# First queries of the attention computed inside the last z tile, and the decays of the second and third quarter two score pairs later

## The reference

```python
def odd_mixer(h_ctx, h_lat, w_in, w_out, conv_w, conv_b, wq, wk, wv, w_if, b_if, norm_g, skip):
    xm, zg = jnp.split(h @ w_in, [ML_WIDTH], axis=-1)          # 2048 + 2048 columns
    xcv = jax.nn.silu(centred_dwconv(xm, conv_w, conv_b))
    q, k, v = headwise(xcv, wq), headwise(xcv, wk), headwise(xm, wv)   # 4x4 blocks
    hm = prefix_bidir(mlstm_scan, (q, k, v), forward, backward)
    return ((head_norm(hm, norm_g) + skip * xcv) * jax.nn.silu(zg)) @ w_out

# one chunk of mlstm_scan; b is the running sum of log f
dmat = where(mask, b[t] - b[s] + log_i[s], -inf)
s    = (q @ k.T) * exp(dmat - m_t)
num  = s @ v + (carried state);  den = sum(s) + (carried state)
h    = num / max(|den|, exp(-m_t))
```

## Time and profile before

| | |
|---|---|
| time, three runs | 2762.35, 2759.66, 2761.38 us; median 2761.38 |
| the profiled execution's own time | 2756.0 us |
| its span | 2754.4 us |
| TensorE busy | 2570.5 us (93% of the span) |
| VectorE, ScalarE, GpSimd busy | 1534.2 (56%), 829.9 (30%), 982.6 (36%) us |
| chain that ended last | TensorE 70%, VectorE 8%, ScalarE 4%, issue 2%, DMA 2%, GpSimd 1% |
| mean granted TensorE clock | 0.974 |
| attention (1905 to 2500 us) | TensorE busy 568.90 of 595.00 us |

### The profile page before, as it was taken

The page is one execution under the profiler, slowest core; times in us unless marked ns, Lnnn a source line. Parts: engine busy times, 40 slices in busy tenths (PEclk is TensorE's granted clock), DMA queues, the critical chain, the costliest instruction groups (busy, mean ns, idle before and its releaser), DMA issues.

```text
span 2754.4 us, 37624 instructions
## 1 busy us (share of the span) xinstructions
PE 2570.5 (93%) x13319; PEld 1990.4 (72%) x13319; DVE 1534.2 (56%) x2362; ACT 829.9 (30%) x997; POOL 982.6 (36%) x1163
## 2 busy tenths in 40 slices
PE   7897789999989998989999999999999989999998
PEld 3777754445445667878877877778888889887787
DVE  4677755887875224433237655866455554646510
ACT  2425634362552113222122111213233242322210
POOL 0139967887800000011233333444334433331000
PEclk9999999999999999999999999999999999999999
DMA  8312220101105776351132333474121220315421
GB/s 298 109 65 99 98 74 24 58 23 50 50 28 191 250 223 215 82 193 35 43 84 83 124 126 116 167 248 146 43 104 62 104 81 31 125 42 168 131 92 46
DMA packets 257472, 298.09 MB, mean 108 GB/s; under 512 B 34960, under 2 KB 217528, under 8 KB 256960
## 3 DMA queue, kind: packets, MB, share of 16 engines
q1 hardware_dynamic: 201568, 206.60, 23.6%
q10 hardware_dynamic: 51168, 73.04, 7.4%
q0 software_dynamic: 4608, 16.78, 1.8%
HBM read 203.09 MB, written 93.29 MB: 108 GB/s over the span
## 4 chain that ended last, share of the span: by engine, by line
PE 70%; DVE 8%; ACT 4%; issue 2%; DMA 2%; POOL 1%; ACTq 0%; DVEq 0%; SPq 0%; POOLq 0%
PE ps L135 61%; PE ps L1315 6%; DVE xc_part L2440 1%; PE ps L973 1%; ACT arena L1510 0%; ACT L1510 0%; PE ps L1320 0%; DVE arena L520 0%; PE ps L1268 0%; POOL decays L2839 0%; PE ps L1146 0%; DVE arena L2204 0%; DMA y_chunks<-arena 0%; DVE s_scan_tmp L2152 0%; DVE arena L2154 0%
## 5 line engine op out<-in xcount | busy, mean ns | idle before, releaser
L135 PE MATMUL ps<-h_full,weights 128*128 128x512 f32 (+1 forms) x1152 | 424.1, 529 | 21.0 <-DMA weights<-in_e_w_in 8.1
L135 PE MATMUL ps<-h_part,in_weight_parts 128*128 128x512 f32 (+1 forms) x1920 | 413.8, 376 | 14.2 <-DVE arena L2357 6.7
L135 PEld LDWEIGHTS ps<-h_part,in_weight_parts 128*128 128x128 f32 x1920 | 337.8, 190 | 85.7 <-issue 13.6
L135 PEld LDWEIGHTS ps<-h_full,weights 128*128 128x128 f32 x1152 | 220.8, 193 | 217.4 <-issue 204.5
L135 PE MATMUL ps<-v_part,p_part 128*128 128x512 f32 x1248 | 296.7, 397 | 0.1
L135 PEld LDWEIGHTS ps<-v_part,p_part 128*128 128x128 f32 x1248 | 235.4, 191 | 49.8 <-issue 0.9
L135 PE MATMUL ps<-q_part,xc_part 128*128 128x256 f32 x1920 | 246.9, 287 | 14.7 <-DVE v_part L2440 10.8
L135 PEld LDWEIGHTS ps<-q_part,xc_part 128*128 128x128 f32 x1920 | 236.5, 194 | 16.4 <-DVE v_part L2440 11.5
L135 PE MATMUL ps<-arena,weights 64*16 64x128 f32 (+2 forms) x896 | 180.7, 395 | 16.5 <-ACT arena L1510 14.4
L1315 PE MATMUL ps<-wo_part,mx_part 128*128 128x512 f32 x768 | 183.8, 400 | 6.9 <-DVE mx_part L2440 6.3
L1315 PEld LDWEIGHTS ps<-wo_part,mx_part 128*128 128x128 f32 x768 | 145.6, 191 | 41.3 <-issue 6.5
(11 more groups left out here) (398 smaller groups left out, 4198.0 us busy)
## 6 DMA issues: line engine op xcount, KB each, us to landing
weights<-in_e_w_in SPq DMA_DIRECT2D x32, 512.0 KB, 4.2
weights<-in_o_w_in SPq DMA_DIRECT2D x32, 512.0 KB, 4.5
s_out_maps<-arena ACTq DMA_DIRECT2D x16, 640.0 KB, 2.9
arena<-s_out_maps SPq DMA_DIRECT2D x16, 640.0 KB, 4.9
ml_xcv<-arena ACTq DMA_DIRECT2D x16, 640.0 KB, 3.0
xc_full<-ml_xcv SPq DMA_DIRECT2D x4, 2560.0 KB, 9.2
xm_tiles<-ml_xm SPq DMA_DIRECT2D x16, 640.0 KB, 3.9
weights<-in_mod_w POOLq DMA_DIRECT2D x17, 512.0 KB, 5.3
```

What stands on the lines that cost most here:

```text
L135: return nc.tensor.matmul(o, lhsT, rhs, start=(k == 0), stop=(k == n - 1))
```

## The change

Three things are moved; no arithmetic is added or taken away.

1. TensorE computes `queries(0, 0)`, 12 matmuls of 256 columns, inside `output_gate(15)`, ahead of its last two blocks k = 6 and 7 (12 matmuls of 512 columns). Before, they followed the tile. ScalarE and VectorE evict these two query halves ahead of their work on tile 15, where before they did it behind that tile's stores. `queries(0, 1)` still follows the tile. To allow it the helper functions are defined ahead of the loops, and the wait for the last z tile's eviction moves to the first `value_sums`.
2. In every head `decays(i, 1)` moves from `first_queries` to behind the third pair of quarter 0.
3. In every head `decays(i, 2)` moves from behind the fifth pair of quarter 0 to behind the third pair of quarter 1.

```diff
--- before.py
+++ after.py
@@ TensorE, output_gate(m)
                 for k in range(DT):
+                    if m == MT - 1 and k == 6:
+                        pe.wait_ge(*past("z_ev", 14))
+                        queries(0, 0)
@@ TensorE, value_sums
+                if u0 and j == 0:
+                    pe.wait_ge(*past("z_ev", MT))
@@ TensorE, behind the z tiles
-            pe.wait_ge(*past("z_ev", 14))
-            queries(0, 0)
             queries(0, 1)
-            pe.wait_ge(*past("z_ev", MT))
             head(0, False)
@@ ScalarE
             for m in range(MT):
+                if m == MT - 1:
+                    queries_high(0, 0)
                 output_gate(m)
...
             def first_queries(i):
-                queries_high(i, 0)
+                if not (isinstance(i, int) and i == 0):
+                    queries_high(i, 0)
                 queries_high(i, 1)
                 act.wait_ge(*past("ce_ready", i + 1))
                 nc.scalar.activation(cE, cE, ACT.Exp).then_inc(sem("cx_ready"), 1)
                 decays(i, 0)
-                decays(i, 1)
...
                 for p in range(NPR - 1):
                     value_high(i, p + 2)
                     weights_high(i, 0, p)
+                    if p == 2:
+                        decays(i, 1)
                 queries_high(i, 2)
                 weights_high(i, 0, NPR - 1)
-                decays(i, 2)
                 value_high(i, 6)
                 for p in range(NPR):
                     value_high(i, p + 7)
                     weights_high(i, 1, p)
+                    if p == 2:
+                        decays(i, 2)
@@ VectorE
             for m in range(10, MT):
+                if m == MT - 1:
+                    for h in range(2):
+                        query_low(0, 0, h)
                 gate_tile(m)
...
                 for q in range(2):
                     for h in range(2):
-                        query_low(i, q, h)
+                        if q or not (isinstance(i, int) and i == 0):
+                            query_low(i, q, h)
```

More of the change, by code:

```diff
@@ L1164, in gate_rows_spread @@
                 last.then_inc(sem("gates_spread"), 1)
[L1166 to L1187, removed]
             def slot(i, *x):
@@ L1300, in head @@
                 weight_sums(i, 3, 1)
-            pe.wait_ge(*past("z_ev", 14))
-            queries(0, 0)
+            mixer_input(1, 0)
+            gate_sums(0, 0)
+            with pe.Fori(1, MT // 2 - 1) as i:
+                mixer_input(i, 1)
+                gate_sums(i - 1, 1)
+                mixer_input(i + 1, 0)
+                gate_sums(i, 0)
+            mixer_input(MT // 2 - 1, 1)
+            gate_sums(MT // 2 - 2, 1)
+            for m in range(MT):
+                output_gate(m)
+                if m == 9:
+                    pe.wait_ge(*past("z_ev", 9))
+                    pe.wait_ge(*past("rows_ready", 2))
+                    pe.wait_ge(*past("em_ready", 1))
+                    for j in range(LBLK):
+                        nc.tensor.transpose(ps[:, 5, 64 * j:64 * j + 64], rA[0:64, P * j:P * j + P], ident[0:64, 0:64])
+                    pe.wait_ge(*past("yr_ready", 1))
+                    for b in range(NBLK):
+                        nc.tensor.transpose(psf[:, 6 * BANK + 64 * b:6 * BANK + 64 * b + 64], rB[0:64, P * b:P * b + P], ident[0:64, 0:64])
+                    pe.wait_ge(*past("tr_ready", 1))
+                    mm(ps[:, 2, 0:40], ones[0:64, :], TR.rearrange("p d h j -> p (d h j)"), 0, 1).then_inc(sem("rows_t"), 1)
             queries(0, 1)
-            pe.wait_ge(*past("z_ev", MT))
             head(0, False)
@@ L1727, in maps_high, with queries_high @@
                 high(CH, CR, "c_high")
+            def queries_high(i, q):
+                for h in range(2):
+                    act.wait_ge(*past("lo_mm", slot_done(i, "q", q, h)))
+                    high(Qs[0][:, q % 2, 2 * h:2 * h + 2].rearrange("p k t -> p (k t)"), slot_bank("q", q, h), "vq_high", MD ** -0.5)
             for m in range(MT):
+                if m == MT - 1:
+                    queries_high(0, 0)
                 output_gate(m)
@@ L1767, in value_high @@
                 high(Vs_[0][:, bs, P * k:P * k + P], slot_bank("v", n)[:, 0:w].rearrange("p (b c) -> p b c", c=P), "vq_high")
[L1769 to L1772, removed]
             def decays(i, q):
@@ L2468, in out_weights_split, with query_low @@
                     out_weights_low(k)
+            def query_low(i, q, h):
+                dve.wait_ge(*past("vq_high", 20 * i + EVICTED["q", q, h]))
+                o, hi = (Qs[x][:, q % 2, 2 * h:2 * h + 2].rearrange("p k t -> p (k t)") for x in (1, 0))
+                V.scalar_tensor_tensor(out=o, in0=slot_bank("q", q, h), scalar=MD ** -0.5, in1=hi.bitcast(F32), op0=ALU.mult, op1=ALU.subtract).then_inc(sem("vq_ev"), 1)
             for m in range(10, MT):
+                if m == MT - 1:
+                    for h in range(2):
+                        query_low(0, 0, h)
                 gate_tile(m)
@@ L2475, in _ @@
                     maps_low(0)
[L2477 to L2480, removed]
             def first_queries(i, then=()):
```

## The result

The changed kernel takes 2737.95 us (median of 4 runs, 2736.18 to 2742.87), beside 2760.52 for the kernel before on the same chip (4 runs, 2758.59 to 2762.35). The ratio is 0.9922, 95% interval 0.9907 to 0.9938: 21.5 us won (17 to 26). The forecast was 16.2 us won and 2745.2, range 2742 to 2752. The profiled execution of after took 2739.68 us. One later run of the kernel before, 4288.94 us at a mean granted clock of 0.556, is a run in a slow state and is left out of every comparison; all others were fast.

What follows compares the result with a forecast made beforehand. TensorE, busy 93% of the span, was taken as the bound, so only its waits and low clock could be won. 2.6 + 10.75 + 0 + 2.83 = 16.2 us off 2761.4 gave 2745.2, range 2742 to 2752.

Steps and rivals of the forecast that it cites:

- The start: Start of head 0: value slot 2 starts 2.6 us earlier, despite a new 4.0 us wait for value rows.
- Rival 1: The start of head 0 gives nothing, TensorE's wait only turning to value rows: 13.6 us won, 2747.8; chance 0.12.
- (b) waits: TensorE's waits for value slot 6 before quarter 1's second score pair, every head; all four go, 10.75 us.
- Rival 4: The (b) waits stay, slot 6 waiting for something the decays hid; only the start is won, 2758.8; chance 0.06.
- Decays of quarter 1: Moved ahead of value slot 5, with a table load in heads 1 to 3: cost 0, 0.76 us left.
- Rivals 3 and 5: Table switch in heads 1 to 3 costs more, 14.6 us won, chance 0.05; moved decays stand bare, +15 us, 0.04.
- (c) waits: TensorE's 1.28 us before quarter 1's first pair, heads 1 to 3, until a query half is evicted; forecast to stay.
- The clock: Two slow score pairs behind (b) waits return to 3.14 us: 2.83 us won, bounds 2.83 and -4.2.
- rival 2: The clock isn't won back, or drops elsewhere: 13.4 or 9.2 us won, 2748.0 to 2752.2; chance 0.13.

Runs made afterwards that it cites:

- start_d1: The kernel before with parts 1 and 2 of the change together, decays of quarter 2 left as before: 2756.03 us, ratio 0.9989.
- p_d2: The kernel before with only part 3 of the change, decays of quarter 2 moved in every head: 2742.40 us, ratio 0.9941.
- fill_b: The kernel before with 16 unread matmuls of 256 columns into an unused bank in each (b) wait: 2752.97 us, ratio 0.9980.
- p_null: The kernel before, unchanged, timed against itself and profiled a second time: 2758.68 us, ratio 1.0000.
- p_again: The changed kernel, unchanged, timed once more beside the kernel before: 2741.12 us, ratio 0.9929.
- p_again2: The changed kernel, unchanged, timed yet again beside the kernel before: 2736.91 us, ratio 0.9924.
- c_only: The kernel before with VectorE evicting both query halves of quarter 2 ahead of the second mixing product, heads 1 to 3: 2761.64 us, ratio 1.0014.
- x2: The changed kernel with c_only's edit, plus half of each head's last value sums ahead of the waiting weight sums: 2730.49 us, 0.9895 to the kernel before.
- p_d1: The kernel before with only part 2 of the change, decays of quarter 1 moved: 2757.64 us, ratio 0.9994.

## Why the prediction was wrong in size and right in kind

1. *The start, 2.6 us.* Right, step by step: a new wait of 3.86 us (4.0 forecast) for value rows that land after 5.1 us (5.3), value slot 2 earlier by 2.8 in the profile, 3.0 by start_d1. Rival 1 (nothing) would have given start_d1 a ratio of 1.0000, just outside its interval; the traces refute it more clearly, by 2.8 to 2.9 us in every execution with parts 1 and 2.
2. *The (b) waits, 10.75 us.* Right that all four go, in after and in p_d2, but worth 11.7: I added up the idle times, and each wait also cost the 0.25 us by which the next group would have started ahead of the end of the one before. Rival 4 is refuted.
3. *Decays of quarter 1, cost 0.* Right, with 0.75 us left where 0.76 was forecast, and no loss behind the table load. Rivals 3 and 5 are refuted: no wait ahead of slots 5 or 10, (c) waits still 1.28.
4. *The clock, 2.83 us with 2.83 as its upper bound.* This step failed: "With the (b) waits gone I take the two slow pairs back to 3.14: 1.49 + 1.34". The (b) waits cost 5.5 us of clock (3.0 to 8.0, fill_b). The single execution that I read had a low clock behind two waits of four, and p_null, the same code, had it behind three, at up to 2.35 us a time. I had even noted that equal waits met the clock differently, and used that only as a reason for a smaller gain: rival 2 lowers the term, and nothing raises it. The price could have been bounded from above by the rows at hand: four waits each followed by a slow pair at 1.34 to 1.49 us, twice 2.83 or 5.7. What is shown is that 2.83 was too small to be a bound; how much too small is open between the profiles' mean of 3.65 and 8.0.
5. *The base.* The forecast of 2745.2 stood on a median of three runs, 2761.4; 62 later runs of the same kernel gave medians of 2758.3 to 2758.6. That is 2.9 us of the 7.25 by which the forecast was off. The other 4.4 lie in the gain, 20.7 against 16.2: 2.7 in the clock (by fill_b; 0.8 by the profiles' mean), 1.0 in the tails of the (b) waits, 0.4 in the start, and 0.4 left over. That is inside the intervals (p_d2 and start_d1 add up to 19.3, each give or take 3 to 4), so whether the parts help one another stays open.

The extra 3.2 us that the profile of after showed in the value sums is no part of this: the profiles of p_again and p_again2 have them slow in heads 0 to 2, at ratios of 0.9929 and 0.9924.

## What to carry to other kernels

A wait on TensorE costs its length, here 0.25 us more than its idle time shows, and, in some executions, the low clock behind it. Price it from the start of one group to the start of the next. For the clock, take that price from several executions or from an experiment that fills the wait, and let the range reach up to every such wait paying in full. Before removing a wait, ask what sets its end and that of the next one: c_only took 3.9 us out in front of waits whose ends were fixed, and lost 3.9; x2 won nothing in head 3, where another engine's chain ended the next wait. A forecast of an absolute time needs more than three runs of the kernel before.

## What the runs showed of the hardware

- Work that nobody reads made the kernel 5.5 us faster (fill_b), by holding the granted clock up across four waits of 2.5 to 3.3 us; 0.55 to 1.36 us of idle time in each did no harm.
- A wait of 1.57 us was followed by the low clock more often than not. In after, the last value sums of heads 0 and 1, 39 matmuls each behind such a wait (start, us):

```profile
2047.40 10.72 PE L135 MATMUL ps<-v_part,p_part 128*128 128x512 f32 x39
...
2204.86 9.11 PE L135 MATMUL ps<-v_part,p_part 128*128 128x512 f32 x39
```

The same matmuls take 10.72 or 9.11 us. In p_null, p_d1, p_d2 and p_again heads 0 to 2 all had the long form (10.70 to 10.74 us), in after only head 0 of these. Over the 12 profiled executions that keep the wait it is 30 of 36. No pair behind a (c) wait of 1.28 to 1.37 us was slow.
- TensorE has waits for nothing the profile shows at the start of head 2, the second turn of a loop: 0.62 us before, 2.35 in after, 0.71 in p_again, which is the same code as after, and 3.33 in x2. Mostly they cost nothing. VectorE has one there too, ahead of its eviction of value slot 0, 1.98 us before:

```profile
2227.39 0.17 DVE L2577 COPY s_scan_tmp<-param_cols 128x16 f32 x1 [1.98 <-issue]
```

Value slot 2 then waits for VectorE (2.06 us before), and the two waits of TensorE together are 2.67 to 2.71 us in ten executions, however they are split (2.89 in after). What sets them was not tried.
